# Norm sums with six of eight square chunks added by GpSimd, and modulation rows turned by transpositions, in a two-layer Mamba-2/GLA and gated-DeltaNet backbone

## The chip, the core and the metric

One core of a Trainium2 chip runs the whole program in one launch. The metric is the device time in microseconds. The kernel before took 1953.9 us (median of 3 runs, 1952.24 to 1958.18). The profile comes from one further execution of it.

## What is computed

Two trunk layers over 256 latent tokens and a prefix of 256 context tokens, width 1024, in fp32, and a last norm over the latent tokens. Cut to what matters here:

```python
for i in range(DEPTH):                       # DEPTH = 2
    sh1, sc1, g1, sh2, sc2, g2 = split(silu(c) @ mod_w[i] + mod_b[i], 6)      # and the same from c_ctx
    hl = rms_norm(x, norm_mix[i]) * (1.0 + sc1) + sh1
    yc, yl = even_mixer(...) if i % 2 == 0 else odd_mixer(...)                # SSD + GLA heads, or gated DeltaNet
    x = x + g1 * yl
    x = x + g2 * swiglu(rms_norm(x, norm_ffn[i]) * (1.0 + sc2) + sh2, w1, w3, w2)
    # the context stream does the same with its own modulation, except in the last layer
return rms_norm(x, final_norm)               # rms_norm: x * rsqrt(mean(x*x) + eps) * w
```

So there are five norms. The kernel calls them mix0, ffn0, mix1, ffn1 and fin. The first three cover 512 columns (context and latent tokens), the last two 256 (latent tokens only).

## The kernel before

The stream `xT` lies transposed: 8 chunks of 128 features on the partitions, with the tokens in the free dimension (128x512 per chunk). Every engine has its program written out by hand, with semaphores between them. No scheduler sets an order. Weights come through a ring that SyncE fills.

**The norm of a chunked stream.** The last product before a norm yields the stream's chunks two at a time. Before ffn0 and ffn1 that product is an output projection (`gemm_and_norm`, four groups g of two chunks each). Before mix1 and fin it is the SwiGLU down projection (`down`, four groups g of three parts each). That one is done with seven products instead of eight per group of tiles; VectorE builds sums of weights for it (the `TENSOR_TENSOR` instructions `ws_sb<-ring_sb`). For chunk c:

- VectorE adds the product to `xT` (`SCALAR_TENSOR_TENSOR xT_sb<-...`).
- ScalarE squares the chunk into `wide[:, c % 2]` and raises `square` (`ACTIVATE wide_sb<-xT_sb`). Before that it waits for `square_used`, which says that the square two chunks back has been read.
- TensorE multiplies a 128x128 matrix of ones with the square and adds into PSUM bank 5 (`norm_sum`, line 1022, `MATMUL psum<-wide_sb,const_sb`). After eight of these, bank 5 holds the sum over all 1024 features on each partition.
- ScalarE then takes Ln and Exp into `wide[:, 2]` (the reciprocal root), VectorE scales the chunks, and the next stage's products start.

TensorE does the sums of chunks 2g-2 and 2g-1 behind group g of the output projection, or behind part 1 of group g of the down projection. The sums of the last two chunks come at the very end, and in front of the next stage stand four matmuls that do nothing but keep the engine running (`keep_clock`).

**The modulation rows.** silu(c) and silu(c_ctx) times 512 columns of `mod_w` leave two rows for each of four slices of the contraction, at partitions 32k and 32k+1 of a bank. ScalarE copies the bank to SBUF (`late_row` or `mod_piece`). TensorE turns four 128x128 pieces of it with `pick`, a 128x2 matrix that adds the four slices, into 8 columns of PSUM (`late_columns` line 844, `mod1_columns` line 1010). VectorE adds the bias and writes `mod` (`late_taken` line 2348, `mod1_taken` line 2354). This occurs 8 times in layer 0 and 12 times for layer 1; the latter lie between the parts of GLA (4) and of the DeltaNet recurrence (8).

GpSimd makes decay matrices for the SSD scan early on, then rests until the DeltaNet stage. A matmul in fp32 leaves two records in the profile; the program's lists further down count it once.

Of the kernel before, what the change touches and what calls it, by code (L numbers as in the profile page):

```python
# [7 lines left out]
P = 128  # L8
# [325 lines left out]
def backbone(nc, x_in, w_in, cols_in, rows_in, gate_in, const_in, out):  # L334
    plan = make_plan()
    ctx = ExitStack()
    with ctx:
# [27 lines left out]
        def cm(name, i=0):  # L365
            return const[:, CI[name] + i, :]
# [446 lines left out]
        def _(pe):  # L813
            def mm(o, l, r, start=True, stop=True, **kw):
                return nc.tensor.matmul(o, l, r, start=start, stop=stop, **kw)  # L815
# [28 lines left out]
            def late_columns(q):  # L844

                pe.wait_ge(S["late_copied"], q + 1)
                if q > 0:
                    pe.wait_ge(S["late_taken"], q)
                for t in range(4):
                    last = mm(psum[:, 5, 2 * t:2 * t + 2], late_row[:, t * P:(t + 1) * P], cm("pick")[:, 0:2])  # L850
                last.then_inc(S["late_columns"], 1)
# [158 lines left out]
            def mod1_columns(q):  # L1010
                pe.wait_ge(S["mod_copied"], q + 1)
                if q > MOD1_EARLY:
                    pe.wait_ge(S["mod_taken"], q)
                for t in range(4):
                    last = mm(psum[:, 7, 2 * t:2 * t + 2], mod_piece[:, t * P:(t + 1) * P], cm("pick")[:, 0:2])
                last.then_inc(S["mod_columns"], 1)

            def keep_clock(n):

                for _ in range(n):  # L1020
                    mm(psum[:, 7, :], ones, cms("ident", 4).rearrange("p a b -> p (a b)"))

# [6 lines left out]
            def gemm_and_norm(stage, src, total, tag, meanwhile=None):  # L1029

                for g in range(D // CB):
                    gemm(stage, g, src, total, lo=NORMS[tag][2] * CTX, meanwhile=meanwhile if g == 0 else None)
                    for c in (2 * g - 2, 2 * g - 1):
                        if c >= 0:
                            norm_sum(tag, c)
                norm_sum(tag, KC - 2)
                norm_sum(tag, KC - 1)
                if tag != "fin":
                    keep_clock(4)
# [333 lines left out]
            def down(i, tag):  # L1373
# [7 lines left out]
                for k in range(DOWN_BLOCKS):  # L1381
# [30 lines left out]
                    if part == 1 and g > 0:  # L1412
                        norm_sum(tag, 2 * g - 2)
                        norm_sum(tag, 2 * g - 1)
                norm_sum(tag, KC - 2)
                norm_sum(tag, KC - 1)
# [356 lines left out]
        def _(act):  # L1773
# [28 lines left out]
            def norm(tag):  # L1802
# [8 lines left out]
                for c in range(KC):  # L1811
# [8 lines left out]
                    if n * KC + c - 1 > 0:  # L1820
                        act.wait_ge(S["square_used"], n * KC + c - 1)
                    own(f(wide[:, c % 2, lo:T], xT[:, tile_no, lo:T], ACT.Square).then_inc(S["square"], 1), S["square"])
# [492 lines left out]
        def _(dve):  # L2315
# [31 lines left out]

            def late_taken(q):
                at = 4 * (MOD_FIRST + q)
                dve.wait_ge(S["late_columns"], q + 1)  # L2350
                own(tt(mod[:, 0, at:at + 4], psum[:, 5, 0:8].rearrange("p (a b) -> p a b", b=2),
                       bc(cl("mod_b", at, 4), 2, 2), ALU.add).then_inc(S["late_taken"], 1), S["late_taken"])

            def mod1_taken(q):
                dve.wait_ge(S["mod_columns"], q + 2)
                own(tt(mod[:, 1, 4 * q:4 * q + 4], psum[:, 7, 0:8].rearrange("p (a b) -> p a b", b=2),
                       bc(cl("mod_b", 48 + 4 * q, 4), 2, 2), ALU.add).then_inc(S["mod_taken"], 1), S["mod_taken"])
# [593 lines left out]
        def _(pool):  # L2951
# [11 lines left out]

            pool.wait_ge(S["decay"], 1)
# [71 lines left out]

            pool.wait_ge(S["beta_lanes"], 1)
# [3 lines left out]
            gdn()  # L3041

# [17 lines left out]
```

## Time and profile before

| what | value |
|---|---|
| median of the runs | 1953.9 us (1952.24 to 1958.18) |
| profiled execution | 1957.48 us |
| its span | 1955.7 us |
| TensorE busy | 1888.6 us, 97% of the span |
| VectorE busy | 984.7 us, 50% |
| ScalarE busy | 580.8 us, 30% |
| GpSimd busy | 102.8 us, 5% |
| DMA engines | 27% of 16 engines' span |

Where the stages lie in the span, in microseconds: first modulation and mix0 norm up to 40, layer 0's projections and SSD to 465, GLA to 600, output projection with norm ffn0 to 714, SwiGLU up to 840 and down to 1123 with norm mix1, layer 1's projections and convolution to 1360, the DeltaNet recurrence to 1660, output projection with norm ffn1 to 1726, SwiGLU to 1943, norm fin to the end. `L815` and `L1777`, `L2320`, `L2323`, `L2956` are the lines of small helpers that issue nearly all instructions of TensorE, ScalarE, VectorE and GpSimd, so that the tiles tell what an instruction is, not its line.

### The profile page before, as it was taken

How to read it: one execution, taken by the hardware profiler on the slowest of the kernel's cores; microseconds unless marked ns; L12 is line 12 of the kernel's file. 1: busy time of each engine (PE TensorE's matmuls, PEld its weight loads, DVE VectorE, ACT ScalarE, POOL GpSimd, SP SyncE). 2: the span in 40 equal slices, each digit the busy share in tenths (PEclk: the TensorE clock that was granted, in tenths of full speed). 3: DMA queues.
4: the chain of work that ended last, by engine and by line, in shares of the span. 5: the costliest groups of instructions: out<-in, count | busy, mean ns of one | idle time of the engine just before them, and what ended most of it. 6: DMA issues, size and time to landing. Idle time of an engine off the chain costs nothing.

```text
span 1955.7 us, 32367 instructions
## 1 busy us (share of the span) xinstructions
PE 1888.6 (97%) x13388; PEld 1344.3 (69%) x13388; DVE 984.7 (50%) x2002; ACT 580.8 (30%) x1340; POOL 102.8 (5%) x102
## 2 busy tenths in 40 slices
PE   6999999999999999999999999999989998999997
PEld 2444677776664448888888874445666666889997
DVE  2551576202782043445532365556857777056764
ACT  4121223522551021111100041224355777022210
POOL 0000231000000000000000000001211111000000
PEclk9999999999999999999999999999989999999999
DMA  7433101133301212222222231212224201344442
GB/s 293 172 123 135 73 22 44 65 151 124 137 3 43 97 63 76 92 90 90 86 76 81 70 124 65 79 65 73 87 88 174 88 2 66 115 144 165 159 163 97
DMA packets 28016, 193.71 MB, mean 99 GB/s; under 512 B 3004, under 2 KB 4285, under 8 KB 5854
## 3 DMA queue, kind: packets, MB, share of 16 engines
q1 hardware_dynamic: 27826, 191.51, 27.0%
q8 instruction: 106, 1.74, 0.4%
q14 instruction: 40, 0.33, 0.1%
q10 hardware_dynamic: 44, 0.14, 0.0%
HBM read 190.59 MB, written 1.05 MB: 98 GB/s over the span
## 4 chain that ended last, share of the span: by engine, by line
PE 89%; DVE 5%; ACT 3%; issue 1%; DMA 1%; POOL 0%; SPq 0%; ACTq 0%; DVEq 0%; POOLq 0%
PE psum L815 88%; DVE ws_sb L2320 2%; DVE gl_tmp_sb L2320 1%; ACT ws_sb L1777 1%; ACT arena_sb L1777 1%; DMA arena_sb<-w 1%; DVE ws_sb L2323 1%; ACT wide_sb L1777 0%; PE psum L1074 0%; DVE xT_sb L2323 0%; PE psum L1223 0%; ACT const_sb L1777 0%; PE psum L1234 0%; DVE ws_sb L2800 0%; DVE ws_sb L2801 0%
## 5 line engine op out<-in xcount | busy, mean ns | idle before, releaser
L815 PE MATMUL psum<-hT_sb,ring_sb 128*128 128x512 f32 (+3 forms) x1600 | 487.6, 456 | 1.1 <-ACT hT_sb L1777 1.1
L815 PEld LDWEIGHTS psum<-hT_sb,ring_sb 128*128 128x128 f32 (+1 forms) x1600 | 277.3, 189 | 194.3 <-issue 178.4
L1777 ACT ACTIVATE ws_sb<-psum 128x256 f32<-128x256 f32 (+5 forms) x373 | 164.6, 443 | 786.8 <-PE psum L815 775.5
L815 PE MATMUL psum<-arena_sb,ws_sb 128*128 128x256 f32 (+3 forms) x2064 | 345.1, 319 | 1.7 <-DVE hT_sb L2320 0.9
L815 PEld LDWEIGHTS psum<-arena_sb,ws_sb 128*128 128x128 f32 (+1 forms) x2064 | 289.7, 182 | 37.2 <-issue 12.7
L815 PE MATMUL psum<-arena_sb,ring_sb 128*128 128x256 f32 (+2 forms) x1200 | 293.9, 397 | 3.1 <-ACT arena_sb L1777 1.7
L815 PEld LDWEIGHTS psum<-arena_sb,ring_sb 128*128 128x128 f32 x1200 | 205.0, 192 | 83.5 <-issue 61.7
L815 PE MATMUL psum<-ring_sb,hT_sb 128*128 128x256 f32 (+3 forms) x1248 | 240.6, 372 | 0.1
L815 PEld LDWEIGHTS psum<-ring_sb,hT_sb 128*128 128x128 f32 (+1 forms) x1248 | 194.1, 176 | 52.9 <-issue 21.2
L2320 DVE TENSOR_TENSOR ws_sb<-ws_sb,psum 128x256 f32<-128x256 f32 (+2 forms) x218 | 87.6, 408 | 131.4 <-ACT ws_sb L1777 71.4
L2320 DVE TENSOR_TENSOR ws_sb<-ring_sb 128x512 f32<-128x512 f32 x132 | 89.2, 676 | 84.0 <-PE psum L815 80.0
L2323 DVE SCALAR_TENSOR_TENSOR ws_sb<-ws_sb,cols_sb 128x512 f32<-128x512 f32 (+1 forms) x176 | 123.7, 703 | 6.3
L2323 DVE SCALAR_TENSOR_TENSOR xT_sb<-psum,mod_sb,xT_sb 128x256 f32<-128x256 f32 x24 | 11.6, 484 | 162.5 <-PE psum L815 162.2
L815 PE MATMUL psum<-const_sb,arena_sb 64*128 64x256 f32 (+5 forms) x576 | 84.9, 394 | 5.1 <-ACT ws_sb L1777 2.0
L1777 ACT ACTIVATE arena_sb<-psum 128x512 f32<-128x512 f32 x56 | 33.5, 598 | 183.9 <-PE psum L815 182.7
L2956 POOL TENSOR_TENSOR wide_sb<-small_sb,const_sb 128x512 f32<-128x512 f32 x24 | 25.9, 1079 | 1106.7 <-DVE arena_sb L2329 1045.3
L1777 ACT ACTIVATE wide_sb<-xT_sb 128x512 f32<-128x512 f32 (+1 forms) x40 | 21.8, 545 | 198.5 <-PE psum L815 126.0
L815 PE MATMUL psum<-wide_sb,const_sb 128*32 128x256 f32 (+2 forms) x384 | 72.4, 447 | 7.4 <-ACT wide_sb L1777 3.2
L815 PEld LDWEIGHTS psum<-const_sb,arena_sb 64*128 64x128 f32 (+3 forms) x576 | 45.9, 177 | 41.5 <-issue 26.7
L2320 DVE TENSOR_TENSOR arena_sb<-ws_sb 128x256 f32<-128x256 f32 (+1 forms) x84 | 30.1, 358 | 86.5 <-ACT ws_sb L1777 85.1
L815 PE MATMUL psum<-ws_sb 128*32 128x32 f32 (+4 forms) x1872 | 65.4, 214 | 0.6 <-issue 0.6
L815 PE MATMUL psum<-hT_sb,ws_sb 128*128 128x256 f32 (+1 forms) x336 | 62.1, 328 | 1.0 <-ACT ws_sb L1777 1.0
(191 smaller groups left out, 1869.7 us busy)
## 6 DMA issues: line engine op xcount, KB each, us to landing
ring_sb<-w SPq DMA_DIRECT2D x146, 1024.0 KB, 4.8
hT_sb<-w SPq DMA_DIRECT2D x16, 1024.0 KB, 4.8
arena_sb<-w SPq DMA_DIRECT2D x8, 1024.0 KB, 19.0
ring_sb<-w SPq DMA_DIRECT2D x8, 768.0 KB, 4.0
xT_sb<-x SPq DMA_DIRECT2D x1, 2048.0 KB, 9.8
const_sb<-consts SPq DMA_DIRECT2D x1, 2048.0 KB, 10.5
y<-xT_sb SPq DMA_DIRECT2D x1, 1024.0 KB, 4.8
ring_sb<-w SPq DMA_DIRECT2D x2, 256.0 KB, 4.0
```

Source lines behind the costliest of these rows:

```text
L815: return nc.tensor.matmul(o, l, r, start=start, stop=stop, **kw)
L1777: return nc.scalar.activation(o, i, func, **kw)
L2320: return V.tensor_tensor(o, a, b, op)
L2323: return V.scalar_tensor_tensor(out=o, in0=a, scalar=sc, in1=b, op0=op0, op1=op1)
L2956: return G_.tensor_tensor(o, a, b, ALU.mult)
```

## The change

For the norms ffn0, mix1, ffn1 and fin, chunk 0 is squared into `wide[:, 2]`, and GpSimd adds the squares of chunks 1 to 5 to it, one at a time. TensorE now sums three tiles for a norm instead of eight: this total, and chunks 6 and 7, all behind the last group. mix0 is left as it was. ScalarE's wait now follows GpSimd's additions. `late_columns` and `mod1_columns` transpose the four pieces against the identity matrix (128 columns each) in place of the products with `pick`, and VectorE adds the four slices with a `tensor_reduce` that reads 32 values of PSUM per partition, and then adds the bias in a second instruction.

```diff
-                    last = mm(psum[:, 5, 2 * t:2 * t + 2], late_row[:, t * P:(t + 1) * P], cm("pick")[:, 0:2])
+                    last = nc.tensor.transpose(psum[:, 5, t * P:(t + 1) * P], late_row[:, t * P:(t + 1) * P], ident)
...
+            def norm_total(tag):
+
+                lo = NORMS[tag][2] * CTX
+                pe.wait_ge(S["square_used"], NORM_AT[tag][0] * KC + KC - 3)
+                mm(psum[:, 5, lo:T], ones, wide[:, 2, lo:T], start=True, stop=False).then_inc(S["square_used"], 1)
+                for c in (KC - 2, KC - 1):
+                    pe.wait_ge(S["square"], NORM_AT[tag][0] * KC + c + 1)
+                    mm(psum[:, 5, lo:T], ones, wide[:, c % 2, lo:T], start=False, stop=(c == KC - 1)).then_inc(S["square_used"], 1)
...
-                    for c in (2 * g - 2, 2 * g - 1):
-                        if c >= 0:
-                            norm_sum(tag, c)
-                norm_sum(tag, KC - 2)
-                norm_sum(tag, KC - 1)
+                norm_total(tag)
...
-                    if part == 1 and g > 0:
-                        norm_sum(tag, 2 * g - 2)
-                        norm_sum(tag, 2 * g - 1)
-                norm_sum(tag, KC - 2)
-                norm_sum(tag, KC - 1)
+                norm_total(tag)
...
-                    if n * KC + c - 1 > 0:
-                        act.wait_ge(S["square_used"], n * KC + c - 1)
-                    own(f(wide[:, c % 2, lo:T], xT[:, tile_no, lo:T], ACT.Square).then_inc(S["square"], 1), S["square"])
+                    if tag == "mix0":
+                        if c > 1:
+                            act.wait_ge(S["square_used"], c - 1)
+                    else:
+                        act.wait_ge(S["square_used"], n * KC + max(c - 2, 0))
+                    home = wide[:, 2 if c == 0 and tag != "mix0" else c % 2, lo:T]
+                    own(f(home, xT[:, tile_no, lo:T], ACT.Square).then_inc(S["square"], 1), S["square"])
...
-                own(tt(mod[:, 0, at:at + 4], psum[:, 5, 0:8].rearrange("p (a b) -> p a b", b=2),
-                       bc(cl("mod_b", at, 4), 2, 2), ALU.add).then_inc(S["late_taken"], 1), S["late_taken"])
+                m = mod[:, 0, at:at + 4]
+                link(V.tensor_reduce(m, four_rows(5), AX_X, ALU.add))
+                own(tt(m, m, bc(cl("mod_b", at, 4), 2, 2), ALU.add).then_inc(S["late_taken"], 1), S["late_taken"])
...
+            def norm_squares(tag):
+
+                n, lo = NORM_AT[tag][0], NORMS[tag][2] * CTX
+                for c in range(1, KC - 2):
+                    pool.wait_ge(S["square"], n * KC + c + 1)
+                    G_.tensor_tensor(wide[:, 2, lo:T], wide[:, 2, lo:T], wide[:, c % 2, lo:T], ALU.add).then_inc(S["square_used"], 1)
+                    pool.wait_ge(S["square_used"], n * KC + c)
```

`mod1_columns` and `mod1_taken` change in the same way, with bank 7. On GpSimd, `norm_squares("ffn0")` and `norm_squares("mix1")` stand in front of its DeltaNet work, those of ffn1 and fin behind it.

TensorE's list around norm ffn0, the output projection of layer 0 (`arena_sb,ring_sb`), the sums (`wide_sb,const_sb`) and the four keeping matmuls (`const_sb`):

```order
-L815 MATMUL psum<-arena_sb,ring_sb 128x512 x48
-L815 MATMUL psum<-wide_sb,const_sb 128x512 x2
-L815 MATMUL psum<-arena_sb,ring_sb 128x512 x32
-L815 MATMUL psum<-wide_sb,const_sb 128x512 x2
-L815 MATMUL psum<-arena_sb,ring_sb 128x512 x32
-L815 MATMUL psum<-wide_sb,const_sb 128x512 x4
+L1228 MATMUL psum<-const_sb,hT_sb 128x128 x32
+L815 MATMUL psum<-arena_sb,ring_sb 128x512 x112
+L815 MATMUL psum<-wide_sb,const_sb 128x512 x3
 L815 MATMUL psum<-const_sb 128x512 x4
```

The eight sums, of which four stood between the groups, have become three, all behind the last group.

TensorE's list in the down projection of layer 0, the seam between parts 1 and 2 of its last group and the end with norm mix1:

```order
 L815 MATMUL psum<-ws_sb,ring_sb 128x256 x4
-L815 MATMUL psum<-arena_sb,ring_sb 128x256 x4
-L815 MATMUL psum<-wide_sb,const_sb 128x512 x2
-L815 MATMUL psum<-arena_sb,ring_sb 128x256 x3
+L815 MATMUL psum<-arena_sb,ring_sb 128x256 x7
 L815 MATMUL psum<-arena_sb,ws_sb 128x256 x6
 L815 MATMUL psum<-extra_sb,ws_sb 128x256 x3
@@ -587,5 +577,5 @@
 L815 MATMUL psum<-ws_sb,ring_sb 128x256 x3
 L815 MATMUL psum<-arena_sb,ring_sb 128x256 x3
-L815 MATMUL psum<-wide_sb,const_sb 128x512 x2
+L815 MATMUL psum<-wide_sb,const_sb 128x512 x3
```

Three pairs of sums leave such seams, and one sum joins the two at the end.

VectorE's list in front of GLA, before (first) and of the change (second): the last modulation columns of layer 0, the gain made of them, and the clearing of a PSUM bank for which GLA's first product waits:

```order
L2329 COPY extra_sb<-psum 128x4x128
L2320 TENSOR_TENSOR mod_sb<-psum,cols_sb 128x8
L2323 SCALAR_TENSOR_TENSOR gain_sb<-mod_sb,cols_sb 128x16
L2593 MEMSET psum 128x512
```

```order
L2334 COPY extra_sb<-psum 128x4x128
L2360 TENSOR_REDUCE mod_sb<-psum 128x8
L2325 TENSOR_TENSOR mod_sb<-mod_sb,cols_sb 128x8
L2328 SCALAR_TENSOR_TENSOR gain_sb<-mod_sb,cols_sb 128x16
L2603 MEMSET psum 128x512
```

One instruction has come in ahead of the gain, and the same has happened at the 19 other places.

## Rows read from the trace of the kernel before

**Rows 1.** The page's first part: busy time (share) xinstructions.

```profile
PE 1888.6 (97%) x13388; PEld 1344.3 (69%) x13388; DVE 984.7 (50%) x2002; ACT 580.8 (30%) x1340; POOL 102.8 (5%) x102
```

**Rows 2.** The page's fourth part: the chain that ended last, by engine.

```profile
PE 89%; DVE 5%; ACT 3%; issue 1%; DMA 1%; POOL 0%; SPq 0%; ACTq 0%; DVEq 0%; POOLq 0%
```

**Rows 3.** Timeline, norm ffn0, weight loads: start, duration (us), engine, instruction [idle before].

```profile
649.66 0.19 PEld L815 LDWEIGHTS psum<-wide_sb,const_sb 128*128 128x128 f32 x1 [0.24 <-issue]
...
651.38 0.19 PEld L815 LDWEIGHTS psum<-arena_sb,ring_sb 128*128 128x128 f32 x1 [0.24 <-issue]
```

**Rows 4.** Timeline, the end of norm ffn0.

```profile
708.73 1.00 DVE L2323 SCALAR_TENSOR_TENSOR xT_sb<-psum,mod_sb,xT_sb 128x256 f32<-128x256 f32 x2 [5.86 <-PE psum L815]
...
710.45 0.63 ACT L1777 ACTIVATE wide_sb<-xT_sb 128x512 f32<-128x512 f32 x1 [0.23 <-PE psum L815]
```

**Rows 5.** Timeline, the end of norm mix1: its last two sums.

```profile
1123.53 1.12 PE L815 MATMUL psum<-wide_sb,const_sb 128*128 128x512 f32 x2 [1.25 <-ACT wide_sb L1777]
...
1124.90 1.12 PE L815 MATMUL psum<-wide_sb,const_sb 128*128 128x512 f32 x2 [0.25 <-ACT wide_sb L1777]
```

**Rows 6.** Timeline, norm ffn1: first update and square, a pair of sums, the end.

```profile
1676.94 0.48 DVE L2323 SCALAR_TENSOR_TENSOR xT_sb<-psum,mod_sb,xT_sb 128x256 f32<-128x256 f32 x1 [15.43 <-PE psum L815]
1677.51 0.42 ACT L1777 ACTIVATE wide_sb<-xT_sb 128x256 f32<-128x256 f32 x1 [4.45 <-DVE xT_sb L2323]
...
1708.61 1.03 PE L815 MATMUL psum<-wide_sb,const_sb 128*128 128x256 f32 x4
...
1709.48 13.98 PE L815 MATMUL psum<-arena_sb,ring_sb 128*128 128x256 f32 x64
...
1723.56 0.48 DVE L2323 SCALAR_TENSOR_TENSOR xT_sb<-psum,mod_sb,xT_sb 128x256 f32<-128x256 f32 x1 [2.97 <-PE psum L815]
1724.00 0.86 ACT L1777 ACTIVATE wide_sb<-xT_sb 128x256 f32<-128x256 f32 x2 [13.81 <-PE psum L815]
```

**Rows 7.** Timeline, the end of norm fin: its last two sums.

```profile
1943.68 1.54 PE L815 MATMUL psum<-wide_sb,const_sb 128*128 128x256 f32 x4 [0.99 <-ACT wide_sb L1777]
```

**Rows 8.** Timeline, TensorE: convolution tile turned by transpositions; modulation piece turned by `pick`.

```profile
71.01 1.04 PE L1074 MATMUL psum<-const_sb,ws_sb 128*128 128x128 f32 x8
...
71.89 1.45 PE L815 MATMUL psum<-hT_sb,ring_sb 128*128 128x512 f32 x3
...
168.54 0.95 PE L815 MATMUL psum<-const_sb,wide_sb 128*128 128x2 f32 x8
...
169.42 1.04 PE L815 MATMUL psum<-ring_sb,small_sb 128*2 128x512 f32 x8
```

**Rows 9.** Timeline, in front of GLA.

```profile
465.46 0.17 DVE L2320 TENSOR_TENSOR mod_sb<-psum,cols_sb 128x8 f32<-128x8 f32 x1 [15.08 <-PE psum L815]
...
466.65 1.71 PE L815 MATMUL psum<-const_sb,arena_sb 64*128 64x448 f32 x4 [1.30 <-DVE psum L2593]
```

**Rows 10.** Groups of VectorE by form: busy us, mean ns | idle before.

```profile
L2584 DVE TENSOR_REDUCE wide_sb<-wide_sb 128x64 f32<-128x448 f32 x8 | 7.5, 936 | 0.3
...
L2580 DVE TENSOR_REDUCE wide_sb<-wide_sb 128x64 f32<-128x384 f32 x8 | 6.6, 820 | 0.3
```

**Rows 11.** Groups of GpSimd by form.

```profile
L2956 POOL TENSOR_TENSOR hT_sb<-hT_sb,arena_sb 128x512 f32<-128x512 f32 x4 | 5.1, 1273 | 53.7 <-ACT small_sb L1777 53.4
```

**Rows 12.** Timeline, GpSimd and VectorE side by side in the DeltaNet stage.

```profile
1381.26 6.05 POOL L2956 TENSOR_TENSOR const_sb<-const_sb,ws_sb 128x256 f32<-128x256 f32 x8
...
1384.31 0.77 DVE L2320 TENSOR_TENSOR ws_sb<-ws_sb,gl_tmp_sb 128x192 f32<-128x192 f32 x1
...
1388.43 0.40 DVE L2320 TENSOR_TENSOR ws_sb<-ws_sb,gl_tmp_sb 128x231 f32<-128x231 f32 x1
```

**Rows 13.** Timeline, VectorE in the down projection of layer 0: first of four weight sums.

```profile
1029.64 0.56 DVE L2320 TENSOR_TENSOR ws_sb<-ring_sb 128x384 f32<-128x384 f32 x1 [7.59 <-PE psum L815]
```

**Rows 14.** Windows: us, PE, PEld, DVE, ACT, POOL busy (x), clock, DMA share, GB/s.

```profile
40.00:200.00 160.00, 158.86 (x499) 72.13 (x500) 66.43 (x109) 35.39 (x63) 2.08 (x2) 1.00 0.37 141
...
1400.00:1445.00 45.00, 39.40 (x666) 31.39 (x664) 36.10 (x83) 16.68 (x23) 4.19 (x5) 0.90 0.23 89
```

More of the change, by code:

```diff
@@ L1014, in mod1_columns @@
                 for t in range(4):
-                    last = mm(psum[:, 7, 2 * t:2 * t + 2], mod_piece[:, t * P:(t + 1) * P], cm("pick")[:, 0:2])
+                    last = nc.tensor.transpose(psum[:, 7, t * P:(t + 1) * P], mod_piece[:, t * P:(t + 1) * P], ident)
                 last.then_inc(S["mod_columns"], 1)
@@ L2346, in modulation0, with four_rows @@
                 mix_gain(0)
+            def four_rows(bank):
+                return psum[:, bank, :].rearrange("p (t c r) -> p t r c", c=4, r=32)[:, :, 0:2, :]
             def late_taken(q):
@@ L2350, in late_taken @@
                 dve.wait_ge(S["late_columns"], q + 1)
-                own(tt(mod[:, 0, at:at + 4], psum[:, 5, 0:8].rearrange("p (a b) -> p a b", b=2),
-                       bc(cl("mod_b", at, 4), 2, 2), ALU.add).then_inc(S["late_taken"], 1), S["late_taken"])
+                m = mod[:, 0, at:at + 4]
+                link(V.tensor_reduce(m, four_rows(5), AX_X, ALU.add))
+                own(tt(m, m, bc(cl("mod_b", at, 4), 2, 2), ALU.add).then_inc(S["late_taken"], 1), S["late_taken"])
             def mod1_taken(q):
                 dve.wait_ge(S["mod_columns"], q + 2)
-                own(tt(mod[:, 1, 4 * q:4 * q + 4], psum[:, 7, 0:8].rearrange("p (a b) -> p a b", b=2),
-                       bc(cl("mod_b", 48 + 4 * q, 4), 2, 2), ALU.add).then_inc(S["mod_taken"], 1), S["mod_taken"])
+                m = mod[:, 1, 4 * q:4 * q + 4]
+                link(V.tensor_reduce(m, four_rows(7), AX_X, ALU.add))
+                own(tt(m, m, bc(cl("mod_b", 48 + 4 * q, 4), 2, 2), ALU.add).then_inc(S["mod_taken"], 1), S["mod_taken"])
             def norm(tag):
@@ L3035, in gdn @@
                     own(tt(o, o, bc(stat[:, 16 + 4 * g:20 + 4 * g], 2, P)).then_inc(S["gated_last"], 1), S["gated_last"])
+            norm_squares("ffn0")
+            norm_squares("mix1")
             pool.wait_ge(S["beta_lanes"], 1)
@@ L3041, in _ @@
             gdn()
+            norm_squares("ffn1")
+            norm_squares("fin")
 def kernel(**inputs):
```

## The prediction

> **What bounds the kernel now.** I read the page's first part first. TensorE is busy for 1888.6 us, 97% of the span, and no other engine is busy for much more than half of the span [rows 1]. The chain of waits says the same from the other side: 89% of the chain that ended last is TensorE, 5% VectorE, 3% ScalarE [rows 2]. So what matters is what TensorE issues, and the few places where it stands still for another engine. An instruction taken from TensorE's list shortens the run by its full pace unless the next instruction must then wait. An instruction added elsewhere costs nothing unless TensorE waits right behind it. After the page I read the timeline at the four norms that change, then the waits around the modulation rows, then the places where GpSimd and VectorE work side by side.
>
> **The price of a norm sum.** A busy time is a poor measure of a pipelined matmul, so I take the distance between weight loads. A pair of sums over 512 columns begins with its first load at 649.66, and the first load of the next group of products is at 651.38 [rows 3]. The pair costs 1.72 us, one sum 0.86. A pair over 256 columns takes the place from 1708.61 to 1709.48, 0.87 us [rows 6].
>
> **Norm ffn0.** The pairs for chunks 0, 1 and 2, 3 stand between groups, with TensorE busy on both sides. Both go: 2 x 1.72 = 3.44 us. The other four sums come behind the last group. There the end is set by a chain. VectorE updates the last two half chunks from 708.73 to 709.73. The square of chunk 7 starts only at 710.45 [rows 4], because the square of chunk 6 had stood behind the sum of chunk 4, which used the same buffer. After the change chunk 6 is squared as soon as it is there, some 6 us earlier, since GpSimd freed the buffer during the group before. Chunk 7's square then follows its own update. ScalarE starts 0.09 us behind such an update (1676.94 + 0.48 to 1677.51 in norm ffn1 [rows 6]), so at 709.82 on the old time axis, 0.63 us earlier. TensorE needs 2 x 0.86 us from the end of the products for the total and chunk 6, and is free before that square ends. The end gains 0.63. Sum for ffn0: 3.44 + 0.63 = 4.07 us.
>
> **Norm mix1.** Three pairs stand inside the down projection, one each in groups 1, 2 and 3: 3 x 1.72 = 5.16 us. At the end TensorE stands still for 1.25 us before the sum of chunk 6, waiting for the square, and again for 0.25 us before that of chunk 7 [rows 5]. The new sum of GpSimd's total (0.86 us) has nothing to wait for and fits into the 1.25 us. The end neither gains nor loses. 5.16 us.
>
> **Norm ffn1.** Two pairs between groups: 2 x 0.87 = 1.74 us. At the end VectorE's last update runs from 1723.56 to 1724.04, and the two squares start together at 1724.00 and end at 1724.86 [rows 6], so the second starts at 1724.43. Without the wait for chunk 4's sum it starts at 1724.13, 0.30 us earlier. 2.04 us.
>
> **Norm fin.** Three pairs over 256 columns in the second down projection: 3 x 0.87 = 2.61 us. The end again has room: TensorE stands still for 0.99 us before its last two sums [rows 7], and the new one needs 0.43.
>
> Together 4.07 + 5.16 + 2.04 + 2.61 = 13.88 us. That is 20 sums fewer on TensorE; all ten pairs between products count in full, and what was at the ends was partly wait.
>
> **GpSimd's additions.** There are five for each of four norms. The nearest row is a GpSimd operation on two SBUF tensors of 128x512, 1.27 us [rows 11]; for 256 columns about half. The squares come in twos, so two additions take some 2.5 us, and then nothing comes until the next group. The groups of the output projection in ffn0 are about 29 us apart (rows 3 and 4 lie two groups apart, 649.66 and 708), those of ffn1 some 15 us. The last addition, of chunk 5, thus ends more than 10 us before the total is read. ScalarE waits for the addition of chunk 4 before it squares chunk 6, done just as long. I take zero. Behind a waiting ScalarE stand the copies of the down projection's products, for which TensorE waits within a few microseconds: this cover is gone only if an addition took more than ten times its row.
>
> What the additions do to VectorE is the open point. In the DeltaNet stage an addition of 192 columns took 0.77 us while GpSimd's row of operations was running (1381.26 to 1387.3), and one of 231 columns took 0.40 us when GpSimd was only clearing memory [rows 12]. So a VectorE instruction with two SBUF inputs can be held up for about 0.4 us by a GpSimd one that reads. The page "SBUF — State Buffer" of the Trainium skill, section "Who interferes with whom", states this as a lock on a shared port pair: such an instruction and a GpSimd instruction that reads SBUF exclude each other for the whole instruction. The trace agrees, with 0.77 against 0.40 us. In the down projections GpSimd's additions fall beside VectorE's weight sums, which it takes up in fours as soon as it has updated the stream. They are prepared one part ahead: VectorE stood idle for 7.59 us before the batch at 1029.64, waiting for TensorE to release a buffer [rows 13]. Two additions of 1.27 us can put the batch before it off by 2.5 us at most, which the 7.59 us cover. In the output projections VectorE has hardly any work. Bounds: 0, and ten additions in the down projections with their full time on the path, 5 x 1.27 + 5 x 0.64 = 9.6 us. I take 0, by the idle time.
>
> **The modulation rows.** On TensorE, eight records of transpositions take from 71.01 to 71.89 until the next product starts, and eight records with the two columns of `pick` take from 168.54 to 169.42 [rows 8]: 0.88 us both. The pace is that of loading the piece, not that of the moving columns. Zero, 20 times.
>
> On VectorE, a reduction is added at each of 20 places. No row shows one of 32 values in PSUM. The two reductions of 384 and 448 values take 820 and 936 ns [rows 10], 1.81 ns a value, so 125 ns are fixed, and 32 values would take about 183 ns. The instruction it stands before read PSUM in 0.17 us [rows 9]. With a gap of 0.03 I take 0.21 us. Below it can't come out under 0; above, the 0.82 us of the smaller reduction is the bound. One of the 20 is on the path for sure: in front of GLA the columns, the gain and the clearing of a bank follow each other on VectorE, and TensorE stands still for 1.30 us behind them [rows 9]. 0.21 us. Of the other 19, seven lie beside long projections with VectorE waiting for TensorE, and twelve in GLA and DeltaNet, where VectorE is busier. I let a quarter of those twelve through: 3 x 0.21 = 0.6 us. Together 0.8 us lost.
>
> **The sum.** 13.9 - 0.8 = 13.1 us. The profiled execution took 1957.48 us, of which 1955.7 is its span, so it would become 1944.4. It lies 3.6 us above the median of the runs; from 1953.9 the same difference gives **1940.8 us**.
>
> **The rivals.**
>
> - *Reductions on the path.* All 20 cost TensorE their time, because in GLA and DeltaNet the small products alternate with VectorE's. For it speaks the wait in rows 9; against it, that TensorE is busy for all but a few microseconds of those stages. 20 x 0.21 = 4.2 us lost, 1944.2 us. Had each the 0.82 us of the bound, it would be 16.4 lost, and 1956.4.
> - *GpSimd holds up the weight sums.* The lock of rows 12 bites in both down projections and TensorE waits for each addition. 9.6 us more lost: 1950.4, no measurable change. The 7.59 us speak against it.
> - *Freed time turns into a wait.* In the down projections TensorE reaches the products that wait for VectorE's additions or for weights earlier, and the six pairs there (5.16 + 2.61 us) were cover. Then 7.8 us are lost: 1948.6. The waits in the middle of those stages are zero in the trace, and the same idle time speaks against it.
> - *The clock falls in the DeltaNet recurrence*, the rival on the slower side. From 1400 to 1445 the granted clock was 0.90 of full [rows 14]: a fifth of that window, 9 us, ran at 1.2 instead of 2.4 GHz. Eight modulation pieces are turned in this stage. The page "TensorE: Matmul & The Clock Gate", Part 4, states that a transposition does not count as busy for the clock in the way a matmul does. If the recurrence ran at the lower level for longer, half of that time would be lost. It decides from 39 us on: then 19.5 us are lost, the gain of 13.1 and the 5.9 of a measurable change are eaten up, and the time is 1960 or more. Against it: in the window from 40 to 200, in which convolution tiles are turned like that at 71.01 [rows 8], the clock was 1.00 [rows 14], and a piece takes 0.88 us among much else.
>
> **How the numbers follow.** What a measurement can tell from no change is about 0.3%, 5.9 us. The forecast has 0.73, the reductions 0.12, the lock 0.05, the wait in the down projections 0.05, the clock 0.03; 0.02 are left for something unseen. Faster by more than 5.9 us (below 1948.0) are the forecast and most of the reductions' case, and a small part of the rest: 0.88. Within it: 0.09. Slower: 0.03. The range reaches down to 1937, which is all reductions hidden (1940.0) and 3 us for the scatter of the runs, of which the lowest was 1.7 us under the median. Up it takes in the reductions' case at twice its estimate (8.4 us lost, 1948.4), so to 1948.
>
> **What would show it.** In the new profile, TensorE's records should be fewer by 40 and its busy time by about 14 us less a pace's difference. The stretch from the first product of each output or down projection to the next stage's first product should be shorter by 4.1, 5.2, 2.0 and 2.6 us. No wait of TensorE should name GpSimd's `wide_sb` in these stretches. Weight sums beside additions should take up to twice as long (0.56 us for 384 columns), with idle time still behind them. The reduction should take about 0.18 us, and the wait of 1.30 us in front of GLA grow to 1.5. The forecast is wrong if the sum of stage differences is under 8 us, if a wait for VectorE or ScalarE appears inside a down projection, or if the windows of the DeltaNet stage show a lower clock than before.

## The result and the profile after

The changed kernel takes 1933.4 us (median of 4 runs, 1930.07 to 1937.44), the kernel before beside it 1954.8 us (4 runs, 1952.24 to 1958.18). The ratio is 0.989, 95% interval 0.9866 to 0.9915: faster, by 21.4 us at the medians. The forecast was 1940.8 us with a range down to 1937. The direction was right, the size some 7 us short, outside the range.

The profiled execution took 1933.88 us with a span of 1932.1, against 1957.48 and 1955.7 before. The page's first part and the engines' shares of the chain, which answer to [rows 1, 2]:

```profile
PE 1866.8 (97%) x13268; PEld 1326.2 (69%) x13268; DVE 996.4 (52%) x2022; ACT 580.8 (30%) x1340; POOL 125.0 (6%) x122
```

```profile
PE 88%; DVE 6%; ACT 3%; issue 1%; DMA 1%; POOL 0%; SPq 0%; ACTq 0%; DVEq 0%; POOLq 0%
```

TensorE still bounds the kernel. Its records fell from 13388 to 13268, by 120. The prediction said 40. That one number points at the miss: 80 further records went, four at each of the 20 modulation pieces.

To see where the time went I matched TensorE's instructions of both traces by their order and noted by how much each starts earlier. The change of this shift across a place is what the place gave:

| place | forecast | measured |
|---|---|---|
| norm ffn0 | -4.07 | -4.08 |
| norm mix1 | -5.16 | -5.17 |
| norm ffn1 | -2.04 | -2.05 |
| norm fin | -2.61 | -2.6 to -2.9 |
| 19 of the 20 modulation pieces on TensorE | 0 | -0.35 to -0.39 each, together -7.0 |
| the last piece of the DeltaNet stage | 0 | 0 |
| the wait in front of GLA | +0.21 | +0.22 |
| the other reductions | +0.6 | none found |

These make 20.7 of the 23.6 us between the spans. The other 2.9 us lie in the start of the program (about 1.1 us) and in stretches of lower clock. Neither belongs to the change. Between two executions of the changed kernel the start differed by 0.8 us and the clock's stretches by up to 5 us (last section).

**The norms.** The timeline (start and duration in us, engine, line, operation, out<-in, tile, count [idle before]) at the end of ffn0, which answers to [rows 4]:

```profile
700.93 1.88 PE L815 MATMUL psum<-wide_sb,const_sb 128*128 128x512 f32 x4
...
701.20 1.00 DVE L2328 SCALAR_TENSOR_TENSOR xT_sb<-psum,mod_sb,xT_sb 128x256 f32<-128x256 f32 x2 [5.86 <-PE psum L815]
...
702.29 0.63 ACT L1778 ACTIVATE wide_sb<-xT_sb 128x512 f32<-128x512 f32 x1 [6.24 <-DVE xT_sb L2328]
...
702.97 1.12 PE L815 MATMUL psum<-wide_sb,const_sb 128*128 128x512 f32 x2 [0.16 <-ACT wide_sb L1778]
```

The two sums at 700.93 (GpSimd's total and chunk 6; an fp32 product leaves two records) need no wait. The square of chunk 7 starts 0.09 us behind its own update (701.20 + 1.00 to 702.29), as the prediction's step has it. At the end of mix1, which answers to [rows 5]:

```profile
1108.80 1.02 PE L815 MATMUL psum<-wide_sb,const_sb 128*128 128x512 f32 x2
...
1110.21 1.13 PE L815 MATMUL psum<-wide_sb,const_sb 128*128 128x512 f32 x2 [0.39 <-ACT wide_sb L1778]
...
1111.58 1.12 PE L815 MATMUL psum<-wide_sb,const_sb 128*128 128x512 f32 x2 [0.24 <-ACT wide_sb L1778]
```

The new sum fills 0.86 of the 1.25 us that TensorE had stood still; 0.39 are left, and the end comes no earlier and no later.

**A modulation piece.** The one at 168.54 before the change, which answers to the second part of [rows 8] and to the reduction that no row showed:

```profile
166.26 0.60 PE L850 MATMUL psum<-const_sb,wide_sb 128*128 128x128 f32 x4
...
166.79 1.04 PE L815 MATMUL psum<-ring_sb,small_sb 128*2 128x512 f32 x8
166.97 0.19 DVE L2360 TENSOR_REDUCE mod_sb<-psum 128x8 f32<-128x32 f32 x1 [5.47 <-PE psum L850]
167.19 0.17 DVE L2325 TENSOR_TENSOR mod_sb<-mod_sb,cols_sb 128x8 f32<-128x8 f32 x1
```

A piece is four records now, and the next product starts 0.53 us behind it (166.26 to 166.79). Before, it was eight records and 0.88 us. VectorE's added instruction takes 0.19 us and puts what follows 0.22 us later (166.97 to 167.19).

The last of the 20 pieces gained nothing:

```profile
1538.26 0.66 PE L1015 MATMUL psum<-const_sb,extra_sb 128*128 128x128 f32 x4 [0.82 <-ACT extra_sb L1778]
...
1539.44 1.14 PE L815 MATMUL psum<-const_sb,arena_sb 64*128 64x256 f32 x8 [0.52 <-ACT const_sb L1778]
```

The product behind it starts 1.18 us after the piece (1538.26 to 1539.44), and so it did before the change (1554.26 to 1555.44). It waits for ScalarE, and the records saved became 0.52 us of waiting.

### The profile page after: what moved, and what is told of

Same layout as the page of the kernel before. It is cut to its first block, busy times and chain, and to the rows that moved or that the text cites. A ratio compares the mean times of both kernels' runs of the same rounds, so it can differ in the third digit from the quotient of the medians.

```text
span 1932.1 us, 32187 instructions
## 1 busy us (share of the span) xinstructions
PE 1866.8 (97%) x13268; PEld 1326.2 (69%) x13268; DVE 996.4 (52%) x2022; ACT 580.8 (30%) x1340; POOL 125.0 (6%) x122
## 3 DMA queue, kind: packets, MB, share of 16 engines
q8 instruction: 105, 1.72, 0.4%
## 4 chain that ended last, share of the span: by engine, by line
PE 88%; DVE 6%; ACT 3%; issue 1%; DMA 1%; POOL 0%; SPq 0%; ACTq 0%; DVEq 0%; POOLq 0%
PE psum L815 87%; DVE ws_sb L2325 2%; DVE gl_tmp_sb L2325 1%; ACT ws_sb L1778 1%; ACT arena_sb L1778 1%; DMA arena_sb<-w 1%; DVE ws_sb L2328 1%; ACT wide_sb L1778 1%; PE psum L1079 0%; DVE xT_sb L2328 0%; POOL wide_sb L2966 0%; PE psum L1015 0%; PE psum L1228 0%; ACT const_sb L1778 0%; PE psum L1239 0%
## 5 line engine op out<-in xcount | busy, mean ns | idle before, releaser
L2979 POOL TENSOR_TENSOR wide_sb<-wide_sb 128x512 f32<-128x512 f32 (+1 forms) x20 | 22.1, 1104 | 1013.2 <-ACT wide_sb L1778 1013.1
L815 PE MATMUL psum<-wide_sb,const_sb 128*32 128x256 f32 (+2 forms) x344 | 57.1, 439 | 7.1 <-POOL wide_sb L2966 3.5
L2331 DVE TENSOR_SCALAR ws_sb<-ws_sb,cols_sb 128x512 f32<-128x512 f32 (+1 forms) x44 | 21.1, 478 | 82.0 <-ACT ws_sb L1778 81.3
```

Of the source, the lines that this page charges most:

```text
L2331: return V.tensor_scalar(o, a, s1, s2, op0, op1) if op1 else V.tensor_scalar(o, a, s1, None, op0)
L2979: G_.tensor_tensor(wide[:, 2, lo:T], wide[:, 2, lo:T], wide[:, c % 2, lo:T], ALU.add).then_inc(S["square_used"], 1)
```

## The experiments

Each ratio is to the kernel before, run on the same chip. Shifts are by matched instructions, against the kernel named. The shares rest on these shifts and not on the medians: beside runs 1 to 4 the kernel before took 1951.13 to 1958.36 us in eleven runs, and by the medians run 1 gains 16.2 us and run 2 9.5, together more than the whole change.

**1. Norms alone, pieces back to `pick`.**

```diff
-                    last = nc.tensor.transpose(psum[:, 5, t * P:(t + 1) * P], late_row[:, t * P:(t + 1) * P], ident)
+                    last = mm(psum[:, 5, 2 * t:2 * t + 2], late_row[:, t * P:(t + 1) * P], cm("pick")[:, 0:2])
```

(the same in layer 1's pieces, without the reductions)

> The change with its modulation part undone: the 20 pieces are again turned by products with pick, and VectorE adds the bias in one instruction. Theory (the prediction's norm terms were right, and the missing 8 us come from the pieces): 13.4 us less than before, about 1941, with the stream of TensorE's instructions 4.1 us earlier behind norm ffn0, 5.2 behind mix1, 2.1 behind ffn1 and 2.6 behind fin, and no shift at the pieces. Rival (a norm sum is worth more than its pace, or the new order frees something else): 20 us less, about 1934, as the whole change has it.

Measured 1939.6 us (1937.53 to 1945.88), ratio 0.9925 (0.9909 to 0.994). Against the kernel before, TensorE is 4.08, 5.17, 2.05 and about 2.6 us earlier at the four norms and no earlier at any piece. The norms' part of the forecast was right to 0.02 us where it can be read.

**2. Turned pieces alone, norms as before.**

```diff
-                    last = mm(psum[:, 5, 2 * t:2 * t + 2], late_row[:, t * P:(t + 1) * P], cm("pick")[:, 0:2])
+                    last = nc.tensor.transpose(psum[:, 5, t * P:(t + 1) * P], late_row[:, t * P:(t + 1) * P], ident)
```

> The kernel before with the modulation part alone: 20 pieces turned by transpositions, a reduction more on VectorE for each, the norms untouched. Theory (four transpositions leave four records on TensorE where four products leave eight, so a piece costs 0.53 us in place of 0.88): 20 x 0.35 = 7.0 us less, minus 0.2 in front of GLA, about 1948, in steps of 0.35 us at each piece. Rival, the prediction's own step (same pace, and the reductions cost 0.8 us): 0.8 us more, about 1955.5.

Measured 1946.25 us (1944.51 to 1949.15), ratio 0.9958 (0.9945 to 0.9972): the part that the prediction had at a loss of 0.8 us is a gain. The shifts show it: 0.35 to 0.39 us at 19 pieces, with nothing at the last piece and nothing at the norms.

**3. Full products with the identity instead of transpositions.** Same source, same 128 moving columns, same reduction; only the kind of the instruction differs.

```diff
-                    last = nc.tensor.transpose(psum[:, 5, t * P:(t + 1) * P], late_row[:, t * P:(t + 1) * P], ident)
+                    last = mm(psum[:, 5, t * P:(t + 1) * P], late_row[:, t * P:(t + 1) * P], ident)
```

> The change, but the pieces are turned by ordinary fp32 products with the identity matrix (128 columns), with the same place in PSUM and the same reductions. Theory (the transposition's mode makes the difference): eight records for a piece again, 20 x 0.35 = 7.0 us more than the change or a little more for 128 columns in place of 2, about 1941. Rival (not the mode but where the result lands, or the new reductions, gained the time): no more than 1 us from the change, about 1934.

Measured 1942.42 us (1939.89 to 1945.63), ratio 0.9936 (0.9921 to 0.9951). The same piece in its timeline:

```profile
166.08 1.05 PE L815 MATMUL psum<-const_sb,wide_sb 128*128 128x128 f32 x8
...
167.07 1.04 PE L815 MATMUL psum<-ring_sb,small_sb 128*2 128x512 f32 x8
```

Eight records and 0.99 us, against four and 0.53. What saves the time is the kind of instruction: an fp32 transposition leaves one record here where an fp32 product leaves two. The number of moving columns has a small price of its own: 0.99 against 0.88 us from 2 to 128.

**4. GpSimd's work tripled.**

```diff
+                    link(G_.tensor_tensor(wide[:, 2, lo:T], wide[:, 2, lo:T], wide[:, c % 2, lo:T], ALU.add))
+                    link(G_.tensor_tensor(wide[:, 2, lo:T], wide[:, 2, lo:T], wide[:, c % 2, lo:T], ALU.subtract))
                     G_.tensor_tensor(wide[:, 2, lo:T], wide[:, 2, lo:T], wide[:, c % 2, lo:T], ALU.add).then_inc(S["square_used"], 1)
```

> The change with every GpSimd addition of a square followed by the same subtraction and the same addition, so three operations for one: 3.8 us per chunk of 512 columns. Theory (GpSimd is fully covered, and its hold on VectorE is taken up by VectorE's idle time): no change from the kernel with the change, within 1 us, and no wait of TensorE inside a down projection. Rival (the shared access of GpSimd and VectorE delays the weight sums): with thrice the work TensorE waits for VectorE in both down projections, 5 us or more, about 1939 and up.

Measured 1931.42 us (1929.77 to 1935.65), ratio 0.9884 (0.9868 to 0.9901). No norm moves by more than 0.01 us against the changed kernel. In the middle of ffn0 three operations follow where one was:

```profile
673.46 1.26 POOL L2979 TENSOR_TENSOR wide_sb<-wide_sb 128x512 f32<-128x512 f32 x1 [2.91 <-ACT wide_sb L1778]
674.80 1.27 POOL L2980 TENSOR_TENSOR wide_sb<-wide_sb 128x512 f32<-128x512 f32 x1
676.15 1.27 POOL L2981 TENSOR_TENSOR wide_sb<-wide_sb 128x512 f32<-128x512 f32 x1
```

The price of zero for the additions held with twice their own length added to them.

**5. Each reduction issued twice.**

```diff
+                link(V.tensor_reduce(m, four_rows(5), AX_X, ALU.add))
                 link(V.tensor_reduce(m, four_rows(5), AX_X, ALU.add))
```

> The change with the reduction of each of the 20 modulation pieces done twice on VectorE (0.19 us and a gap of 0.03 each). Theory (only the one in front of GLA is on the path): TensorE's stream is 0.22 us later in front of GLA and no later at the other 19 places; the whole time is within 1 us of the change, about 1934. Rival (in GLA and the DeltaNet stage the reductions hold TensorE up): 12 more places with 0.22 us each, 2.9 us more than the change.

Measured 1932.26 us (1931.4 to 1933.47), ratio 0.9885 (0.9868 to 0.9901). Against the changed kernel TensorE is 0.30 us later by GLA's front, where 0.22 was expected, and nowhere else beyond what the clock does. Of the 20 reductions one is on the path; the three that I let through in GLA and DeltaNet are not.

**6. GpSimd adds all eight chunks.** TensorE makes one sum of the total; chunks 6 and 7 are added like the others.

```diff
-                for c in range(1, KC - 2):
+                for c in range(1, KC):
```

> The change with the squares of chunks 6 and 7 also added by GpSimd, so that TensorE sums one tile for a norm instead of three. Theory (the two sums behind the last group were hidden under the wait for the last square, so taking them away gains nothing, and the addition of chunk 7 comes on the path): 1.27 + 0.1 us more at ffn0 and mix1, 0.73 + 0.1 at ffn1 and fin, 4.4 us more than the change, about 1938. Rival (each sum off TensorE gains its pace): 2 x (1.72 + 0.87) = 5.2 us less than the change, about 1928.

Measured 1943.88 us (1940.42 to 1945.42), ratio 0.994 (0.9925 to 0.9955), some 10.5 us behind the changed kernel. The sign was foreseen, the size (4.4) not. By matched instructions the four norms lose 9.0 us: 2.97, 4.36, 0.86 and 0.83. The last two are what was expected (0.83 each); the first two were expected at 1.37 each. The rest up to 10.5 us lies in the start and in the clock of other stages. At the end of ffn0:

```profile
699.57 0.63 ACT L1775 ACTIVATE wide_sb<-xT_sb 128x512 f32<-128x512 f32 x1 [6.24 <-DVE xT_sb L2325]
700.34 1.26 POOL L2976 TENSOR_TENSOR wide_sb<-wide_sb 128x512 f32<-128x512 f32 x1 [5.60 <-ACT wide_sb L1775]
701.65 1.67 PE L815 MATMUL psum<-wide_sb,const_sb 128*128 128x512 f32 x2 [3.28 <-POOL wide_sb L2976]
703.12 4.79 PE L815 MATMUL psum<-const_sb 128*128 128x512 f32 x8
```

TensorE waits 3.28 us for GpSimd, and then the eight records that keep the clock up take 4.79 us, where the changed kernel has:

```profile
703.93 3.60 PE L815 MATMUL psum<-const_sb 128*128 128x512 f32 x8
```

So ffn0 loses 2.97 us: 1.37 us for the addition of chunk 7, as expected, and some 1.6 us by the lower clock. At mix1 the wait is 5.04 us and the loss 4.36, the same eight records again taking 4.79. There another cause shows, VectorE's update beside GpSimd's addition:

```profile
1110.18 1.91 DVE L2325 SCALAR_TENSOR_TENSOR xT_sb<-ws_sb,mod_sb,xT_sb 128x256 f32<-128x256 f32 x2
1110.55 1.26 POOL L2976 TENSOR_TENSOR wide_sb<-wide_sb 128x512 f32<-128x512 f32 x1 [29.11 <-ACT wide_sb L1775]
```

The same pair of updates took 0.88 us in the changed kernel, so the last square comes 1.03 us later. At ffn1 the wait was shorter, and the eight records behind it kept their 3.60 us:

```profile
1714.08 0.70 PE L815 MATMUL psum<-wide_sb,const_sb 128*128 128x256 f32 x2 [2.01 <-POOL wide_sb L2976]
1714.62 3.60 PE L815 MATMUL psum<-const_sb 128*128 128x512 f32 x8
```

This is why the last two chunks belong on TensorE.

**7. The kernel before with a third square buffer,** to see whether ffn0's 0.63 us at the end come from the buffer alone.

```diff
-                mm(psum[:, 5, lo:T], ones, wide[:, c % 2, lo:T], start=(c == 0), stop=(c == KC - 1)).then_inc(S["square_used"], 1)
+                mm(psum[:, 5, lo:T], ones, wide[:, c % (2 if tag == "mix0" else 3), lo:T], start=(c == 0), stop=(c == KC - 1)).then_inc(S["square_used"], 1)
```

> The kernel before with the squares of the four later norms rotating over three buffers instead of two, and nothing else changed. It tests the end term of the prediction by itself: the last square no longer waits for a sum. Theory: the stage behind norm ffn0 starts 0.6 us earlier and that behind ffn1 0.3 us earlier against the kernel before, mix1 and fin are unchanged, 0.9 us in all. Rival (the ends are set by TensorE's sums): no shift at any norm.

A single execution, 1952.83 us, which tells nothing by its time. By matched instructions ffn0 gained 0.21 us instead of 0.6, ffn1 0.33, the other two nothing. In ffn0 the third buffer alone lets the square start early, but TensorE then has four sums to do:

```profile
706.05 3.60 PE L815 MATMUL psum<-wide_sb,const_sb 128*128 128x512 f32 x8
...
707.41 0.63 ACT L1777 ACTIVATE wide_sb<-xT_sb 128x512 f32<-128x512 f32 x1 [6.24 <-DVE xT_sb L2324]
```

The square is done at 708.04, the sums run to about 709.5. The 0.63 us of the prediction need both: the buffer free and one sum fewer behind the last group (three instead of four).

**8. More turned by transposition** on top of the changed kernel: the first four pieces of layer 0 and the dt rows, with two of VectorE's memory clearings moved ahead.

```diff
-                    for t in range(4 * q, 4 * q + 4):
-                        last = mm(psum[:, 4, 2 * t:2 * t + 2], mod_row[:, t * P:(t + 1) * P], cm("pick")[:, 0:2])
+                    for t in range(4):
+                        last = nc.tensor.transpose(psum[:, 4 + 2 * (q % 2), t * P:(t + 1) * P], mod_row[:, (4 * q + t) * P:(4 * q + t + 1) * P], ident)
...
-                    last = mm(psum[:, 7, j * 32:(j + 1) * 32], dtT[:, j * P:(j + 1) * P], ident[32:64, 32:64])
+                    last = nc.tensor.transpose(psum[:, 7, j * 32:(j + 1) * 32], dtT[:, j * P:(j + 1) * P], ident[32:64, 32:64])
```

> The change with its second part carried on: the first four pieces of the modulation (mod0) are turned by transpositions too, each reduced as it comes; the 32 columns of dt are turned by transpositions instead of products with the identity; and two fills of memory by VectorE (a row of ones before norm mix0, PSUM bank 1 before GLA) are moved ahead of the pieces for which TensorE waits. Theory: 1.0 to 1.4 us less up to the first projection, 0.4 us less at dt, 0.4 to 0.7 less in front of GLA, 2.2 us less than the change in all, about 1931. Rival (the first part is bound by the arriving weights and the inputs): only the 0.8 us behind the first part, about 1932.6.

Measured 1930.16 us (1928.38 to 1933.12), ratio 0.988 (0.9863 to 0.9897). Against the changed kernel 1.7 us came before 56 us and 0.6 by 176 us. Another 3.5 came through GLA, where this execution had no stretch of low clock, so I ran both again (10 and 11).

**9. Each of the 80 transpositions issued twice.**

```diff
-                    last = nc.tensor.transpose(psum[:, 5, t * P:(t + 1) * P], late_row[:, t * P:(t + 1) * P], ident)
+                    for twice in range(2):
+                        last = nc.tensor.transpose(psum[:, 5, t * P:(t + 1) * P], late_row[:, t * P:(t + 1) * P], ident)
```

> The kernel after, with each of the 80 late transpositions of the modulation pieces issued twice, so eight transpositions a piece at 20 pieces. Theory (an fp32 transposition is one pass of about 0.11 us, an fp32 product is two, and the passes set the pace of a piece): each piece takes 4 x 0.11 = 0.44 us longer, 0.53 becoming 0.97 us; 20 x 0.44 = 8.8 us above the kernel after. Rival (a piece costs a fixed time for starting and stopping the stream of products, whatever is in it): the second four would ride along for less than half of that, under 4 us in all.

Measured 1941.94 us (1940.07 to 1944.96), ratio 0.9933 (0.9912 to 0.9955), 7.5 us above the changed kernel on the same chip (1934.45; 8.8 were expected). The piece:

```profile
167.85 1.04 PE L851 MATMUL psum<-const_sb,wide_sb 128*128 128x128 f32 x8
...
168.82 1.04 PE L815 MATMUL psum<-ring_sb,small_sb 128*2 128x512 f32 x8
```

0.97 us instead of 0.53: 0.44 for four transpositions, 0.11 each. It is 0.43 or 0.44 at 19 pieces and nothing at the last, where TensorE waits for ScalarE anyway, 8.3 us in all. Eight transpositions take what eight records of products with the identity took (0.99, run 3). The second four cost nearly as much as the first; the rival is out.

**10 and 11. The changed kernel and that of 8 once more, on one chip.**

> The kernel after once more, beside the next run on the same chip: about 1933 us, as before. If differences in the start and in the clock's low stretches are all that tells such runs apart, the stages of the norms and the pieces agree with the first profile of it to 0.05 us.

> The kernel of e8 once more (the first four pieces and the dt rows also turned by transpositions, VectorE's bank clearing ahead of its wait), beside the kernel after on the same chip. By passes of 0.11 us the first four pieces save 4 x 0.35 = 1.4 us and the dt rows about 0.4: 1.8 us below the kernel after. The rest of the first difference lay in GLA, where that run had no low stretch of the clock; if it was chance, the two are 1.8 us apart or less, if the earlier clearing keeps the clock up, 3 us or more.

The changed kernel took 1934.45 us (1933.15 to 1935.2), ratio 0.9895 (0.988 to 0.9911); the other 1931.35 us (1930.28 to 1932.27), ratio 0.988 (0.9865 to 0.9895). The ranges of the runs don't overlap: 3.1 us faster than the changed kernel, and faster than both kernels of this case. Matched against run 10, the first four pieces gave 1.54 us, the stretch between them and the first projection another 0.42, and the dt rows 0.64, together 2.6 where 1.8 were expected. In that stretch TensorE's wait for the scaled chunks fell from 1.14 to 0.80 us; the row of ones had stood between the gain and the scaling in run 10 (0.48 us at 36.80) and no longer does, which would explain it but was not tried alone. The other moved clearing, of the bank, gave nothing: TensorE waits 1.54 us in front of GLA as it did 1.52, now for the modulation columns instead of the cleared bank.

```profile
460.45 0.48 DVE L2550 MEMSET psum<- 128x512 f32 x1 [15.16 <-ACT arena_sb L1780]
...
461.19 0.17 DVE L2327 TENSOR_TENSOR mod_sb<-mod_sb,cols_sb 128x8 f32<-128x8 f32 x1
...
461.46 1.02 PE L815 MATMUL psum<-const_sb,arena_sb 64*128 64x448 f32 x4 [1.54 <-DVE mod_sb L2327]
```

The clearing, now ahead, takes the same 0.48 us out of the same chain. In the second execution the clock in GLA was lower (0.97 of full from 460 to 520), so the earlier clearing does not hold it up. The remaining 0.5 us between the medians I can't assign.

## Why the prediction fell short, step by step

**The failed step** is the first paragraph on the modulation rows: "0.88 us both. The pace is that of loading the piece, not that of the moving columns. Zero, 20 times." I compared eight records at 71.01 with eight at 168.54 [rows 8] and took each for one group of four turns. At 71.01 the transpositions stand in the code four to a tile, and eight records are two tiles; at 168.54 eight records are one piece, because each fp32 product leaves two. So one turn cost 0.11 us there and 0.22 us here, and the row that I cited for "no difference" showed the factor of two. The counts in the trace before have it too: 104 convolution transpositions (26 tiles of four) left 104 records, the 80 `pick` products left 160. In place of zero the trace has -0.35 to -0.39 us at 19 pieces, -7.0 us; runs 2, 3 and 9 show this by doing it alone, by undoing only the kind of instruction, and by doubling it. The reason given there, that loading the piece sets the pace, is not refuted. TensorE's weight loads fell by the same 120 records (13388 to 13268), so a product loads its piece twice and a transposition once. That the loads set the pace of a record is likely, since 2 and 128 columns differ by so little, but it is not shown. The sum with that term is 13.9 + 7.0 - 0.2 = 20.7 us, and 1953.9 - 20.7 = 1933.2, against 1933.4 measured. That it meets the median so closely is luck: the start and the clock's stretches move single runs by several us, and the median of the kernel before was 1953.7 to 1955.8 us in the other comparisons.

The Trainium skill has a rule here, on the page "Perfetto Trace Analysis", section "Transposes": a logical transposition is to be issued as one and not as a standard matmul, since "Transposes have special mux logic to skip arithmetic for transposes". Run 3 agrees, with 0.53 against 0.99 us. No term rests on it.

**The price of a norm sum**, 1.72 and 0.87 us a pair: right. Run 1 has 1.72 us at each seam of mix1.

**The ends.** ffn0's 0.63 and ffn1's 0.30 us: right to 0.01 in the sum, and run 7 adds that the first hangs on the missing sum as much as on the free buffer. mix1's and fin's ends: neither gain nor loss, right. Fin's end has 0.56 us of waiting left of 0.99, as the 0.43 of the new sum leave.

**GpSimd's additions at zero**: right, and run 4 shows the cover. That a reading GpSimd and a VectorE instruction with two SBUF inputs hold each other up was right too. In the down projection of layer 0:

```profile
1045.40 0.69 DVE L2325 TENSOR_TENSOR ws_sb<-ring_sb 128x512 f32<-128x512 f32 x1
...
1046.23 1.73 POOL L2979 TENSOR_TENSOR wide_sb<-wide_sb 128x512 f32<-128x512 f32 x1 [1.14 <-ACT wide_sb L1778]
1046.86 1.64 DVE L2325 TENSOR_TENSOR ws_sb<-ring_sb 128x512 f32<-128x512 f32 x1
```

This addition takes 1.73 us, others 1.27, and the weight sum beside it takes 1.64 instead of its undisturbed 0.69: they hold each other up by 0.5 to 1.0 us. That is more than the "up to twice as long" of the prediction, and it still cost nothing. No wait of TensorE in these stages names GpSimd, and the only one there for VectorE, 0.22 us at 1849.12, stood in the kernel before too. The times agree with what the prediction cites from the Trainium skill, "SBUF — State Buffer", section "Who interferes with whom".

**The reductions.** 0.19 us for 0.18, and the wait in front of GLA grew from 1.30 to 1.52 us, forecast 1.5:

```profile
461.34 0.19 DVE L2360 TENSOR_REDUCE mod_sb<-psum 128x8 f32<-128x32 f32 x1 [14.73 <-PE psum L850]
...
462.12 0.48 DVE L2603 MEMSET psum<- 128x512 f32 x1 [0.18 <-DVE gain_sb L2328]
...
462.75 0.65 PE L815 MATMUL psum<-const_sb,arena_sb 64*128 64x448 f32 x2 [1.52 <-DVE psum L2603]
```

The quarter of twelve that I let through, 0.6 us, was not there (run 5); that this put the forecast further off is the small part of the miss.

**The rivals.** None came. "Reductions on the path" and "GpSimd holds up the weight sums" fell with runs 5 and 4, "freed time turns into a wait" with the full 1.72 us at each seam, and the clock in DeltaNet was not lower than before beyond what repeats of one kernel differ by (0.97 of full over the stage before, 0.96 after, 0.95 in run 10). What I lacked was a rival on the faster side: the turned pieces had a bound for VectorE's part, and none for TensorE's, although the instruction was as new at its place there as the reduction was on VectorE.

## What to carry to other kernels

Before two groups of records are compared, count from the code what one instruction leaves in the trace. In these traces an fp32 product leaves two records and an fp32 transposition one, at 0.11 to 0.13 us a record for 2 to 128 columns. So turning the rows by transposition cut TensorE's part from 0.88 to 0.53 us a piece and moved the addition of the slices to a reduction on VectorE. An addition moved to GpSimd is free only as long as nobody waits behind it: the additions for six of eight chunks cost nothing even tripled, those for the last two cost 9.0 us at four norms. And where an estimate is "no difference", check it against the count of records it implies (40 here, 120 measured).

## What the runs showed of the hardware

**A wait can cost more than its length, by a lower clock behind it.** In run 6 eight records of 512 columns took 4.79 instead of 3.60 us behind waits of 3.28 and 5.04 us, and 3.60 behind one of 2.01 us, where the granted clock was 1.00. From 695 to 715 us it was 0.91 of full, so about 3.6 of these 20 us ran at 1.2 instead of 2.4 GHz. No run here varies the wait alone. Its windows, and those of the changed kernel (columns: busy us of TensorE, weight loads, VectorE, ScalarE, GpSimd, then the granted clock, the DMA share and GB/s):

```profile
695.00:715.00 20.00, 16.72 (x35) 6.97 (x34) 9.55 (x19) 10.98 (x20) 1.26 (x1) 0.91 0.15 53
```

```profile
695.00:715.00 20.00, 19.84 (x47) 8.50 (x46) 9.12 (x20) 10.84 (x21) 0.00 (x0) 1.00 0.15 53
```

**Stretches of low clock come and go between executions of one kernel.** The changed kernel, in its first profile and then in run 10:

```profile
460.00:520.00 60.00, 56.32 (x966) 33.05 (x966) 39.90 (x101) 30.36 (x68) 0.00 (x0) 0.91 0.38 142
...
1575.00:1605.00 30.00, 28.02 (x508) 20.00 (x508) 17.91 (x52) 26.29 (x67) 0.00 (x0) 1.00 0.27 103
```

```profile
460.00:520.00 60.00, 55.79 (x982) 33.04 (x984) 44.15 (x110) 33.17 (x76) 0.00 (x0) 1.00 0.38 142
...
1575.00:1605.00 30.00, 28.02 (x434) 19.55 (x432) 15.45 (x44) 22.80 (x58) 0.00 (x0) 0.90 0.26 101
```

One lost time in GLA, the other in DeltaNet; by matched instructions some 3.5 us in GLA and 5 in DeltaNet, while at the norms ffn0 to fin and at the modulation pieces the two differ by less than 0.13 us. The start differs by 0.8 us. What starts or ends such a stretch is not shown. A difference of 2 to 3 us between single profiles of two kernels is therefore no finding unless it stands at an instruction that the change touched.
